# ScalarE issues the loads of w2 in the loop of a mixture-of-experts layer, the sync engine those of w1 and w3

## The reference, cut to what matters

```python
for e in range(MOE_EXPERTS):                       # 32
    he = jax.nn.silu(t @ w1[e]) * (t @ w3[e])      # t: 256 x 1024, w1, w3: 1024 x 512
    y = y + gate[:, e:e + 1] * (he @ w2[e])        # w2: 512 x 1024
```

## Time and profile before

| | |
|---|---|
| median of 3 runs | 1407.7 us (1407.22 to 1408.53) |
| the profiled execution | 1407.11 us, its span 1405.3 us |
| TensorE busy | 1157.0 us (82%) |
| VectorE, ScalarE busy | 370.8 us (26%), 264.5 us (19%) |
| HBM read | 451.97 MB |
| granted TensorE clock, mean | 0.933 of full speed |
| loads of MoE units | 192 of 2048 KB, all from SP's queue |

### The profile page before, as it was taken

The page is one execution under the profiler, slowest core; times in us unless marked ns, Lnnn a source line. Parts: engine busy times, 40 slices in busy tenths (PEclk is TensorE's granted clock), DMA queues, the critical chain, the costliest instruction groups (busy, mean ns, idle before and its releaser), DMA issues.

```text
span 1405.3 us, 19968 instructions
## 1 busy us (share of the span) xinstructions
PE 1157.0 (82%) x8298; PEld 646.0 (46%) x8298; DVE 370.8 (26%) x933; ACT 264.5 (19%) x485; POOL 26.5 (2%) x36
## 2 busy tenths in 40 slices
PE   4998797977869678787899999979887877868777
PEld 2665644434334233342587776454442423424332
DVE  2346623111111011110465654241110111101011
ACT  2224312101111011110233444031110101101010
POOL 1012100000000000000000000000000000000000
PEclk9999897999999889998999999979998998989899
DMA  9520083999999999999752235428999999999994
GB/s 346 227 112 0 16 344 149 430 427 429 429 427 430 427 430 428 429 429 427 285 204 90 110 121 209 174 97 367 429 427 430 427 428 430 427 430 427 430 428 205
DMA packets 33645, 453.48 MB, mean 323 GB/s; under 512 B 4888, under 2 KB 5260, under 8 KB 6220
## 3 DMA queue, kind: packets, MB, share of 16 engines
q1 hardware_dynamic: 32092, 452.08, 76.9%
q0 software_dynamic: 288, 0.33, 0.2%
q10 hardware_dynamic: 1232, 0.62, 0.2%
HBM read 451.97 MB, written 1.05 MB: 322 GB/s over the span
## 4 chain that ended last, share of the span: by engine, by line
PE 61%; DMA 28%; DVE 7%; issue 2%; ACT 2%; SPq 0%; ACTq 0%; DVEq 0%; POOL 0%
DMA ring<-in_moe_units 27%; PE bank L668 13%; PE bank L638 12%; PE bank L708 9%; PE bank L658 5%; PE bank L619 4%; PE bank L418 4%; PE bank L822 4%; PE bank L568 2%; PE bank L628 1%; PE bank L426 1%; PE bank L779 1%; DMA vrow<-in_od_conv_b 1%; DVE ys L1488 1%; DVE xT L1473 1%
## 5 line engine op out<-in xcount | busy, mean ns | idle before, releaser
L638 PE MATMUL bank<-ring,xT 128*32 128x256 f32 x4096 | 286.1, 429 | 139.5 <-DMA ring<-in_moe_units 125.6
L638 PEld LDWEIGHTS bank<-ring,xT 128*32 128x32 f32 x4096 | 137.8, 117 | 286.7 <-DMA ring<-in_moe_units 144.4
L668 PE MATMUL bank<-ys,pgT 128*128 128x512 f32 x512 | 236.4, 604 | 14.0 <-DVE ys L1488 14.0
L668 PEld LDWEIGHTS bank<-ys,pgT 128*128 128x128 f32 x512 | 92.0, 189 | 153.7 <-issue 125.6
L708 PE MATMUL bank<-h,ring 128*128 128x256 f32 x576 | 130.4, 382 | 0.0
L1016 ACT ACTIVATE ys<-bank 128x512 f32<-128x512 f32 x64 | 38.3, 598 | 466.6 <-PE bank L658 466.6
L708 PEld LDWEIGHTS bank<-h,ring 128*128 128x128 f32 x576 | 107.3, 190 | 18.6 <-issue 5.1
L1482 DVE COPY heT<-bank 128x128 f32<-128x128 f32 x64 | 18.7, 292 | 287.6 <-PE bank L646 287.6
L1478 DVE TENSOR_TENSOR he<-sg,bank 128x128 f32<-128x128 f32 x64 | 18.4, 288 | 259.2 <-ACT sg L1010 259.2
L1488 DVE COPY ys<-bank 128x512 f32<-128x512 f32 x64 | 44.3, 692 | 137.3 <-PE bank L658 137.3
L658 PE MATMUL bank<-extra,heT 128*32 128x512 f32 x512 | 64.6, 622 | 14.5 <-DVE heT L1482 7.6
(11 more groups left out here) (301 smaller groups left out, 928.7 us busy)
## 6 DMA issues: line engine op xcount, KB each, us to landing
ring<-in_moe_units SPq DMA_DIRECT2D x160, 2048.0 KB, 22.3
extra<-in_moe_units SPq DMA_DIRECT2D x32, 2048.0 KB, 26.5
ring<-in_od_in_units SPq DMA_DIRECT2D x10, 2048.0 KB, 11.2
ring<-in_ev_in_units SPq DMA_DIRECT2D x6, 2048.0 KB, 22.9
ring<-in_od_out_units SPq DMA_DIRECT2D x4, 2048.0 KB, 7.7
ring<-in_ev_out_units SPq DMA_DIRECT2D x2, 2048.0 KB, 9.3
x<-in_x SPq DMA_DIRECT2D x2, 512.0 KB, 6.1
out<-x SPq DMA_DIRECT2D x2, 512.0 KB, 2.7
```

The lines of the kernel that those rows point to most:

```text
L638: last = mm(bank[4 + e % 2][32 * j:32 * j + 32, 0:256], xT[:, 4 * part + k, CAP * e:CAP * e + CAP], w[:, k, :, 256 * (j // 2) + j % 2:256 ...
L668: last = mm(bank[2 * t + h][:, :], pgT[:, e, t, :], ys[:, e % 2, 512 * h:512 * h + 512], start=False, stop=False)
```

## The change

SP's loop issues parts 0 and 1 alone. ScalarE's loop, which ran as often as the group steps, now runs once less, and its body issues the next step's w2 of expert e right behind `take(e)`, on ScalarE's queue; the last step is written out a second time behind the loop, without the loads. The wait at `used` of `take(e)` covers the tile, since `down(e)` was its reader. The first step's loads, ahead of the loop, stay with SP.

```diff
                 with sp.Fori(0, last_step) as i:
                     for e in range(GROUP):
-                        for part in range(3):
+                        for part in range(2):
...
                 act.wait_ge(rt_ok, layer + 1)
-                nr = act.value_load(rounds[0:1, layer:layer + 1], min_val=1, max_val=ROUNDS)
-                with act.Fori(0, nr * NGROUPS) as i:
+                last_step = act.value_load(rounds[0:1, 2 + layer:3 + layer], min_val=NGROUPS - 1, max_val=ROUNDS * NGROUPS - 1)
+                def step(i, more):
                     act.wait_ge(m["pt_ps"], i + 1)
...
                     for e in range(GROUP):
                         silu(e)
                         take(e)
+                        if more:
+                            act.dma_start(moe_memory(layer, e, 2), moew[layer, bass.ds(((i + 1) % NGROUPS) * GROUP + e, 1), 2, :, :]
+                                          .rearrange("e p c -> (e p) c")).then_inc(full[layer][moe_slot(layer, e, 2)], 16)
+
+                with act.Fori(0, last_step) as i:
+                    step(i, True)
+                step(last_step, False)
```

## The result

The change makes the kernel slower: 1419.3 us median of 5 runs (1415.35 to 1422.24), before 1407.7 us; the ratio is 1.0082, with a 95% interval of 1.0057 to 1.0106.

What follows compares the result with a forecast made beforehand. The prediction took DMA bytes at 429 GB/s to bound the loops. All terms were 0 except the tail, 2 x 4.6 = +9.2 us, taking the median from 1407.7 to 1416.9 us; range 1405 to 1425 us.

Steps and rivals of the forecast that it cites:

- The bound: Both MoE loops: DMA engines full at 429 GB/s, share 1.01, a step lasts as long as its bytes; the change moves neither.
- ScalarE's issues cost nothing: ScalarE in each step: four issues of about 0.45 us lie under waits, 0 us; uncovered, 13 us a layer.
- Sharing: Two queues on the same 16 engines: no change in rate taken, bounds -7 to +3 us; w2 at half rate.
- The tail: Each loop's last step: (2, 0) lands 9.8 us later, (3, 0) 4.9 us later; the end moves +4.6 us a layer.
- the case of the dropped clock: Last step: TensorE waits for (2, 0) long enough to lose its clock, up(2, 0) takes 3.64 us; +5.8 us a layer.
- Passed on whole: Between the loops: layer 0's shift reaches layer 1 unchanged, since the next mixer's loads move with it; 2 x 4.6 = +9.2 us.
- A: Rival, both loops: two queues move bytes faster; at 436 GB/s 6 us faster, 1402 us; chance 0.1.
- C: Rival, last step: nothing moves, (2, 0) lands as now or the shift is absorbed; within 3 us, 1408; chance 0.13.
- B: Rival, every step: w2 fetched too early fills all eight tiles and starves the loop; 1429 to 1453 us; chance 0.1.
- the backlog at 1348.33: SP's queue in a step: w2's latest issue is already at 1348.33 and the engines never run dry; evidence against B.

Runs made afterwards that it cites:

- the first experiment: The changed kernel with each loop's last turn undone: there SP issues all twelve units in the old order and ScalarE none; 1408.3 us, ratio 1.0005 to before.

## Why the prediction came out right, point by point

*The bound.* Right: a step of 58.4 us, share 1.01, 429 GB/s, and the last byte at 435.0 us against 434.8. As forecast, the steps ahead of the last one grow and the last one shrinks: in layer 1 the first seven take 409.8 us instead of 396.2, and the last, up to L679, 44.6 instead of 52.9.

*ScalarE's issues cost nothing.* Right, and smaller than taken: 0.34 us each against 0.45. 48 of them in the first experiment give 1.0005. The written-out last step shows no cost either: silu(1) in it comes 1.21 us after take(0), and 1.22 us before the change.

*Sharing.* The units on ScalarE's queue land in 14.0 us. Twice 4.9 and the 2.6 us around a transfer make 12.4, so they move at near half the rate. That a DMA engine takes its queues in turn is a statement of the Trainium skill (DMA: Bandwidth & Descriptors, Queues, rings and completion order); the 14.0 us fit it, but no run here isolates it. SP's units took 24.2 us where they had taken 22.3. That spreading over queues adds no bandwidth is the Trainium skill's as well (DMA: Bandwidth & Descriptors, Rules for kernel authors): the trace agrees, 429 GB/s with one queue and with two.

*The tail.* Right in its mechanism and nearly in its terms. (2, 0) was to land 9.8 us later: it did, 9.8. up(3, 0) was to find its unit there: it did. The term that was off is the one that had been left open, whether TensorE's clock drops at up(2, 0): I took the middle of 4.2 and 5.8. In layer 1 the wait is 2.26 us, inside the 1 to 6 that I had worked out, and the up behind it takes 3.30 us and not 2.02; in layer 0 it is 2.00 us and 2.82. So it was nearer the case of the dropped clock: +5.0 and +5.3 us a layer, against 4.6 taken.

*Passed on whole.* This was mis-sized: the sum put the stretch between the loops at 0, and it grew by 2.2 us. From L679 of layer 0 to layer 1's first product it takes 273.3 us, before 271.0. In the changed kernel ScalarE's last two small issues ahead of the mixer take 0.76 and 0.94 us instead of 0.45, and the first L708 products 5.11 instead of 3.69 us:

```profile
690.88 0.76 ACTq L1034 DMA_DIRECT2D dts<-in_od_A_log  x1
691.67 0.94 ACTq L1035 DMA_DIRECT2D dsk<-in_od_D  x1
692.66 1.57 ACT L1038 ACTIVATE hT<-bank,vT 128x256 f32<-128x256 f32 x4 [10.01 <-issue]
```

```profile
693.28 5.11 PE L708 MATMUL bank<-hT,ring 128*128 128x256 f32 x16 [2.71 <-ACT hT L1038]
```

These are two effects, and the other kernels tell them apart. The slow issues come in the three kernels that put the two w2 ahead of (2, 0) in the last turn, this one, the one-queue kernel with that order and the one with experts 2 and 3 on ScalarE, and in no other; TensorE idles 2.7 to 2.9 us ahead of its first L708 products there, and 1.9 elsewhere, so this part is 0.8 to 1.0 us. The slow products are a lower granted clock, 0.71 here. They come here (5.11 us), in the one-queue kernel with the changed last turn (6.56, at 0.55) and with experts 0 and 1 on ScalarE (5.37, at 0.67), which has the old order at the end; with experts 2 and 3 on ScalarE they take 3.69 at full clock. So this part, 1.4 us here, is not shown to come from the order. The stretch is 274.6, 272.5 and 271.8 us in those three others, and 270.8 in the remaining five. Why the small issues are slower and what takes the clock down stays open. The small issues slow down as the mixer's own loads run out (DMA share 0.98 from 690 to 692 us, 0.30 from 692 to 694); the slow products come at a share of 0.02 here, but of 0.87 with experts 0 and 1 on ScalarE.

Together: 10.2 us in the loops and 2.2 between them, some 12.5 us in this execution, against 9.2 forecast and 11.6 between the medians.

*The rivals.* A (a faster plateau) did not happen: 429 GB/s. C did not: (2, 0) landed 9.8 us later. B as I put it, all tiles full, did not either (share 1.01 in a step), but its neighbour is real and dear: the engines run dry when the one queue stands at a wait while tiles behind it are free. I had named the backlog at 1348.33 as evidence against B and not seen how thin it is: one unit less, and a step costs 4 us more.

## What to carry to other kernels

In a loop that lasts as long as its bytes, who issues a load and when changes nothing in the middle as long as the DMA engines never run dry; what counts is which units land last before the stream ends, and how much work stands behind each of them. Work it out unit by unit, and go on to the next unit once the first is moved, since the gate passes on at once. And know how many units stand in the queue when the issuing engine stops at a wait: a load that is taken off that queue may be the one that bridges the wait.

## What was not expected of the hardware

The size of the gap: from an issue at 1226.07 bytes flow again at about 1227, so a dry queue costs the wait and about a microsecond more, and TensorE runs on at full clock through it. The rest of the 4.4 us a step lies around the gap (413 GB/s in the stretch ahead of it, 270 in the first two microseconds behind it).

And the clock after a short wait: TensorE idled 2.26 us ahead of up(2, 0) in the changed kernel, and the granted clock of the up(2, 0) behind it was 0.57 on average over its 3.30 us, between the two levels and nearer the 1.2 GHz one. After 2.70 us in the kernel before it was 0.58. I had expected a wait near the short end to cost nothing. Nor does the length of the wait settle it: with the last turn undone TensorE idled 2.41 us, and the up behind it took 2.50 us at 0.77; in the changed kernel a wait of 1.92 us at 1321 cost nothing (2.02 us at 1.00). What else decides is not shown.
